# Top-k steps spread differently over the stick-breaking pairs, and the last feed-forward round's ScalarE and VectorE work in another order

## What is computed

```python
h = rmsnorm(x);  proj = h @ w_in                      # q,k,v of two mixers, indexer, two gates
# branch A, stick-breaking attention, 8 heads of 64, strictly causal
z = q @ k.T / 8;  log_beta = log_sigmoid(z)
attn = exp(log_beta + later_sum(log_sigmoid(-z)));  o_sb = attn @ v
# branch B, sparse attention: an indexer scores the keys, top_k(score, 128) of them are kept per query
s = q @ k.T / 8 - slope * dist, others -inf;  o_sa = softmax(s) @ v      # 8 heads on 2 kv heads
merged = sigmoid(g_sb) * (o_sb @ w_sb) + sigmoid(g_sa) * (o_sa @ w_sa);  x = x + merged @ w_out
x = x + square(relu(rmsnorm(x) @ w_ff1)) @ w_ff2       # hidden width 4096
```

## Time and profile before

| | |
|---|---|
| median of 3 runs | 769.47 us (769.15 to 769.64) |
| the profiled execution, its own time | 768.71 us |
| its span (first to last instruction) | 766.9 us |
| TensorE busy | 736.8 us, 96% |
| VectorE busy | 525.6 us, 69% |
| ScalarE busy | 335.2 us, 44% |
| GpSimd busy | 223.7 us, 29% |

### The profile page before, as it was taken

How to read it: one execution, slowest core, us unless ns; L and a number is a source line. 1 busy time by engine, 2 the same in 40 slices (tenths; PEclk the granted TensorE clock), 3 DMA queues, 4 the chain that set the end, 5 groups by cost and what they waited for, 6 DMA issues and landing times.

```text
span 766.9 us, 9737 instructions
## 1 busy us (share of the span) xinstructions
PE 736.8 (96%) x3482; PEld 581.9 (76%) x3482; DVE 525.6 (69%) x730; ACT 335.2 (44%) x477; POOL 223.7 (29%) x193
## 2 busy tenths in 40 slices
PE   8999999999997999899999999999999999999798
PEld 4768778778775555578887888888888888888686
DVE  5354786786797856635664559796877878695672
ACT  5235643355663666842242444433535252535220
POOL 2104425000001455102121046452617080807310
PEclk9999999999999999999999999999999999999999
DMA  9307332310111212113163133333140605031102
GB/s 329 118 15 219 111 103 63 110 56 2 54 56 55 56 55 56 56 54 112 55 221 135 56 110 111 110 106 114 53 166 8 210 0 182 37 109 55 55 15 97
DMA packets 43893, 70.63 MB, mean 92 GB/s; under 512 B 2641, under 2 KB 27217, under 8 KB 43858
## 3 DMA queue, kind: packets, MB, share of 16 engines
q1 hardware_dynamic: 43858, 70.17, 27.7%
HBM read 65.71 MB, written 2.10 MB: 88 GB/s over the span
## 4 chain that ended last, share of the span: by engine, by line
PE 51%; issue 23%; POOL 13%; DVE 9%; ACT 3%; DMA 1%; POOLq 0%; DVEq 0%; SPq 0%; ACTq 0%
POOL a_lo L609 6%; PE ps L415 6%; PE ps L417 6%; PE ps L416 6%; PE ps L408 5%; PE ps L410 5%; PE ps L409 5%; POOL qo_sb L620 2%; POOL qo_sb L622 2%; PE ps L1540 2%; PE ps L1576 1%; DVE cut_lo L399 1%; PE ps L1522 1%; PE ps L1617 1%; PE ps L1691 1%
## 5 line engine op out<-in xcount | busy, mean ns | idle before, releaser
L1691 PE MATMUL ps<-b_hi,cut_hi 128*128 128x512 f32 (+1 forms) x272 | 102.6, 377 | 0.0
L1692 PE MATMUL ps<-b_lo,cut_hi 128*128 128x512 f32 (+1 forms) x272 | 102.4, 377 | 0.0
L1693 PE MATMUL ps<-b_hi,cut_lo 128*128 128x512 f32 (+1 forms) x272 | 102.4, 376 | 0.0
L415 PE MATMUL ps<-cut_hi,a_hi 128*128 128x512 f32 x224 | 90.0, 402 | 0.8 <-DVE a_lo L990 0.8
L417 PE MATMUL ps<-cut_hi,a_lo 128*128 128x512 f32 x224 | 87.6, 391 | 0.0
L416 PE MATMUL ps<-cut_lo,a_hi 128*128 128x512 f32 x224 | 87.4, 390 | 0.0
L399 DVE TENSOR_TENSOR cut_lo<-raw,cut_hi 128x2048 fp32r<-128x2048 f32 (+1 forms) x30 | 58.5, 1951 | 33.9 <-ACT cut_hi L391 33.8
L609 POOL TENSOR_TENSOR a_lo<-qo_sb,a_hi 128x512 fp32r<-128x512 f32 x49 | 78.2, 1626 | 5.6 <-ACT a_hi L868 5.6
L858 ACT ACTIVATE qo_sb<-ps 128x512 f32<-128x512 f32 x32 | 19.2, 599 | 133.1 <-PE ps L1693 88.5
L597 POOL TENSOR_SCALAR qo_sb<-qo_sb 128x128 f32<-128x128 f32 (+3 forms) x28 | 30.2, 1080 | 132.2 <-DVE snmax L1162 131.5
L391 ACT ACTIVATE cut_hi<-raw 128x2048 fp32r<-128x2048 f32 (+1 forms) x30 | 48.7, 1622 | 41.9 <-PE ps L410 23.4
(11 more groups left out here) (192 smaller groups left out, 1657.8 us busy)
## 6 DMA issues: line engine op xcount, KB each, us to landing
raw<-in_w_ff_dram SPq DMA_DIRECT2D x32, 1024.0 KB, 5.5
raw<-in_w_in_dram SPq DMA_DIRECT2D x16, 1024.0 KB, 5.3
gates<-in_x_dram SPq DMA_DIRECT2D x8, 512.0 KB, 6.2
raw<-in_w_out_dram SPq DMA_DIRECT2D x4, 1024.0 KB, 5.1
raw<-in_w_in_dram SPq DMA_DIRECT2D x4, 512.0 KB, 6.9
raw<-in_w_branch_sb_dram SPq DMA_DIRECT2D x2, 1024.0 KB, 5.1
raw<-in_w_branch_sa_dram SPq DMA_DIRECT2D x4, 512.0 KB, 6.2
out_dram<-gates SPq DMA_DIRECT2D x8, 256.0 KB, 2.0
```

The source lines that it names most:

```text
L415: nc.tensor.matmul(dst, l_hi, w_hi, start=start, stop=False)
L1691: T.matmul(dst, w_hi[:, w], b_hi[:, k, a:b], start=(k == 0), stop=False)
L1692: T.matmul(dst, w_hi[:, w], b_lo[:, k, a:b], start=False, stop=False)
L1693: mm = T.matmul(dst, w_lo[:, w], b_hi[:, k, a:b], start=False, stop=(k == KD - 1))
```

## The change

Two separate edits. First, in the stick-breaking stage one top-k step is put before the first pair, and the second call of each pair takes 8, 6, 5, 0 steps instead of 5, 5, 5, 5. No step is dropped: 1 + (2+8) + (2+6) + (2+5) + (2+0) = 28. Second, at the end of g = 6 ScalarE's `last_high(1)` goes from ahead of `hidden_high(1)` and `right_high(S3)` to behind `relu(7, 2)`, and `relu(7, 2)` is put ahead of `last_high(2)`; VectorE's `square(7, 2)` goes ahead of `last_low(1)`, `last_low(2)` ahead of `right_low(A22)`, and the first `add_z` behind `drain(S3)`. TensorE, GpSimd and SyncE keep their lists.

```diff
@@ act_last_end(g) @@
                 last_high(0)
-                last_high(1)
                 hidden_high(1)
                 right_high(g, S3)
+                relu(g + 1, 2)
+                last_high(1)
                 last_high(2)
-                relu(g + 1, 2)
                 hidden_high(2)
                 right_high(g, A22)
                 last_high(3)
@@ the stick-breaking stage on VectorE @@
+            topk(1)
             for c in range(SBH // 2):
                 softplus(2 * c)
                 softplus_cut(2 * c)
...
                 if c == 3:
                     sa_logits(0)
                     sa_logits(1)
-                topk(5)
+                topk((8, 6, 5, 0)[c])
@@ dve_last_end(g) @@
                 last_low(0)
+                square(g + 1, 2)
                 last_low(1)
-                square(g + 1, 2)
                 drain(g, S4)
-                add_z(0, 1, 14 * g + 2 * S4)
+                last_low(2)
                 right_low(g, A22)
                 drain(g, S3)
-                last_low(2)
+                add_z(0, 1, 14 * g + 2 * S4)
                 last_low(3)
```

## The result

| | before | after |
|---|---|---|
| median | 769.56 us (769.15 to 770.36, 4 runs) | 757.94 us (757.77 to 758.00, 4 runs) |
| ratio, 95% interval | | 0.9846 (0.9833 to 0.9858) |
| the profiled execution, its span | 768.71, 766.9 us | 757.77, 755.7 us |
| mean granted clock | 0.996 | 1.0 |

The change makes the kernel 11.6 us faster; 758.3 was forecast.

What follows compares the result with a forecast made beforehand. TensorE, busy 96% of the span, bounds the kernel, so only its two long stops can be won: 5.24 + 5.94 = 11.2 us off the 769.47 us median gives 758.3 us, range 757.4 to 760.0.

Steps and rivals of the forecast that it cites:

- The first stop: Before the sparse attention's first transpose: 4.62 us shrinks to 0.92, the transpose starting 3.70 us earlier, at 241.14.
- The clock term of 1.64: Behind the first transpose: 1.64 us more won if the 0.92 us stop leaves TensorE's clock up.
- the 0.1 that was taken: Top-k steps moved into c=2 make the cast between nothing and 0.5 us late; 0.1 us deducted.
- Rival C: Top-k steps overfill c=1 or c=2, TensorE stops at sum_later: about 0.5 us, at worst 1.5; chance 0.03.
- The second stop: Before S4 at the end of g=6: stop gone, 4.58 us, plus 1.46 of clock; 5.9 for the edit.
- the margin in u = 0: VectorE's chain through square(7,3) to GpSimd's cut is ready 0.5 us before TensorE wants the fourth column.
- Rival B: VectorE's chain is the new end; TensorE stops 0.5 to 1.5 us inside u=0: 758.8 to 759.8; chance 0.09.
- D: Only one edit works, another wait lying hidden under the removed one: 763.6 or 764.3 us; chance 0.03.
- E: Slower than before: a late last slab delays last_low(1) and work behind it; 771.1 us at 19.2 us transfer; chance 0.01.
- My own doubt from it: A single short stop that kept the clock is no proof for another; without the clock's return, 1.64 us less.

Runs made afterwards that it cites:

- d3: The changed kernel with three of the five top-k steps put back at the end of pair c=3; 758.33 us.
- m_chain: The changed kernel with two more 128x512 additions on VectorE right ahead of square(7,3), their results unused; 758.85 us.
- e1: The kernel before with the top-k edit alone; 765.14 us beside 770.25.
- e2: The kernel before with the edit of the last round alone, ScalarE's and VectorE's order both; 763.61 us.
- e3: The kernel before with ScalarE's new order in the last round alone, VectorE's list as it was; 764.42 us.
- e4: The kernel before with VectorE's new order in the last round alone, ScalarE's list as it was; 770.05 us.
- d4_steps: The changed kernel with four of the five top-k steps put back at the end of pair c=3; 761.26 us.
- c_addz: The changed kernel with the first add_z back right behind drain(S4); 757.80 us.

## Why the prediction was right, point by point

**The first stop.** Predicted 241.14 and a stop of 0.92, measured 241.25 and 0.93. The clock term of 1.64 was counted and came, as 1.54 (3.76 less 2.22, and the same by the longer sequence to gate(9)), and the trace of d3 shows that a stop of 1.59 us could have kept it too. 5.24 us were forecast for this edit, 5.13 came.

**Where the top-k steps went.** VectorE after the change, ahead of the softplus of c = 1 and of c = 2, then at the cast of c = 2, for the earlier trace rows:

```profile
177.45 1.49 DVE L1138 SCALAR_TENSOR_TENSOR lg<-ps,lg 128x1280 f32<-128x1280 f32 x1 [1.28 <-ACT lg L762]
...
199.49 1.49 DVE L1138 SCALAR_TENSOR_TENSOR lg<-ps,lg 128x1280 f32<-128x1280 f32 x1 [1.18 <-ACT lg L762]
...
208.05 0.83 DVE L1145 CAST sp_hi<-lg 128x1280 fp32r<-128x1280 f32 x1
```

The softplus of c = 1 starts at 177.45 as before, so the step ahead of c = 0 and the three in it cost nothing. 5.04 us of idle time became 1.28, 2.25 became 1.18, and the 1.29 ahead of the cast are used up, with the cast 0.14 us late. sa_scores(1) starts at 239.83 instead of 239.73: the 0.1 that was taken. Rival C fell.

**The second stop.** Predicted no stop before S4 and 5.44 us to ff1(7,3); so it is. With the 5.17 us by which S4's place in TensorE's list had moved by then (722.15 forecast without the first edit, 716.98 with it), the forecasts were 715.2 for drain(S1), 717.6 for last_high(1) and 729.3 for square(7,3); measured 715.30, 717.68 and 729.66. The last is 0.33 late, the one step that was sized too small: last_low(1) starts at 718.76 (718.7 forecast), but last_low(2) took 1.48 us from start to start beside GpSimd instead of 1.14, and these 0.34 are the whole of it. The forecast had 0.2 for this, and put 0.1 into the sum. So the margin in u = 0 was not 0.5 us but 0.2 (m_chain), and the 0.1 us taken off for it was not lost: there is no stop at L1769, and the edit brought 6.1 us for the 5.94 forecast. Rival B did not come, but it stood near, nearer than its chance of 0.09 says: ScalarE's order alone met it, with a stop of 0.68 us.

**Rivals D and E.** Both edits paid (e1, e2), so D fell. For E, ScalarE waited for no transfer in the changed kernel; what a later landing would have done wasn't tried.

**The sum.** 11.2 us forecast, 11.6 between the medians, 11.2 between the two spans, so the mechanism and its sizes came as forecast. The 0.4 are not in the changed kernel but in the one before, whose runs differ by up to 1.9 us. The traces show where: the time from the first transpose to gate(9), 8.27 at full clock, is 9.81 in the trace before, 10.23 in e2, 10.16 in e3 and 9.48 in e4, behind the same stop of 4.62 us and with the same instructions. From S4 to ff1(7,3), 5.44 at full clock, it is 6.90 before, 7.82 in e1 and 8.20 in e4 (stops of 4.4 to 4.6 us). One stop costs 1.2 to 2.8 us in clock, as it happens. I had taken one trace's 1.46 and 1.64 for the price.

The Trainium skill, "TensorE: Matmul & The Clock Gate", section "What's actually happening", says that the moment of the switch shifts from run to run; these traces agree, by the numbers just given. My own doubt from it, that one short stop proves little for another, did not come true here: in the traces stops of 0.93, 1.03, 1.20 and 1.59 us all kept the clock.

The spread of the runs is a weaker sign. The changed kernel has runs within 0.3 us of each other, but so have `e2_last_only` (763.5 to 763.8) and `d4_steps` (761.1 to 761.4), each with a stop of over 3 us; and `d3_steps`, with none, spreads over 0.8 us.

## What to carry to other kernels

On an engine that works its list in order, ask of each stop what stands ahead of the wanted instruction and when that thing itself is wanted: here five top-k steps not needed for 20 us (the mask that they serve is written at 268.3 in the trace before) and a cut not needed for 19 us each held TensorE for 4.5 us. Put such work where the same engine waits anyway, count its idle gaps first, and follow the queue on both engines, since ScalarE's move without VectorE's left 0.8 us behind. Where the bounding engine is TensorE, count a long stop as its length plus the clock behind it, here 1.2 to 2.8 us.

## What the runs showed of the hardware

The clock's price is a step, not a slope, as far as these traces go: the third step put back cost 0.66 us (stop 1.59 us), the fourth 3.0 us more between the two traces, with the stop at 3.10. Behind stops of 3.1 us and more TensorE lost 1.2 to 2.8 us, differing between traces with the same work, and in d4 the slow matmuls began 1.3 us after the first transpose, not with it.

VectorE and GpSimd got in each other's way where VectorE reads two operands from SBUF: two drains (one operand in PSUM) took 1.27 or 1.28 us, beside GpSimd or not, while two add_z took 1.28, 1.61 or 2.08 us and a 128x1024 cut 1.21 or 1.55. The Trainium skill, "GPSIMD Engine Reference", section "1. Specifications", names this contention for instructions with two SBUF inputs; the traces agree and give it a size. VectorE, then GpSimd, in the trace before, shortly ahead of the end of g = 6:

```profile
711.22 3.37 DVE L1231 TENSOR_TENSOR cut_lo<-raw,cut_hi 128x2048 fp32r<-128x2048 f32 x1
714.51 2.31 DVE L1254 TENSOR_TENSOR home_lo<-raw,home_hi 128x1024 fp32r<-128x1024 f32 x1
```

```profile
712.40 3.34 POOL L633 TENSOR_TENSOR a_lo<-qo_sb,a_hi 128x512 fp32r<-128x512 f32 x1
```

Whichever started second stood until the first had ended. GpSimd's cut, 1.3 us elsewhere, started while VectorE's lay there until 714.59 and took 3.34; VectorE's next, 1.21 elsewhere, then waited for GpSimd, which ended at 715.74, and took 2.31. In the pairs looked at, the second became longer by the time that it lay beside the first, less 0.13 to 0.16 us: 0.80 for 0.93 us (`e3_act_only`), 0.33 or 0.34 for 0.47 (`c_addz`, the changed kernel), 1.10 for 1.23 and 2.04 for 2.19 (the rows above), and in `e4_dve_only` GpSimd's 0.23 for 0.39, where VectorE's cut was first and kept its 1.21. That is why the place of add_z made no difference in `c_addz`: either operation started 0.47 us ahead of the end of GpSimd's cut and waited for that end.
